# Turning the Xx blocks of a triangular inverse on VectorE instead of by TensorE products

## The chip, the cores and the metric

The kernel runs on one core of one Trainium2 chip. Times are device microseconds of that core. The engines are called as in the profile: PE is TensorE's matmul unit, PEld its weight load, DVE is VectorE, ACT is ScalarE, POOL is GpSimd, SP is SyncE.

## What is computed

Two model blocks run one after the other on 512 tokens of width 1024, everything in fp32. The first block (modulated norm, gated spatial unit, state space scan, feed forward) isn't touched by the change. The second block is:

```python
h = rmsnorm(x, norm_gain[l])
z = h @ w_in[l]
...
y_a = multi_scale_pool(u_a, pool_w[l], pool_scale[l])
y_b = rwkv7_time_mix(sh, w0[l], w_up[l], a0[l], a_up[l], k_k[l], k_a[l],
                     r_k[l], gn_gain[l], gn_bias[l]).astype(x.dtype)
y = jnp.concatenate([y_a * jax.nn.silu(g_a), y_b * jax.nn.silu(g_b)], axis=-1)
x = x + y @ w_out[l]
```

rwkv7_time_mix is a recurrence over the tokens for 8 heads of width 64:

```python
sa = jnp.einsum('bhvk,bhk->bhv', state, -kk_t)
state = (state * w_t[:, :, None, :]
         + sa[..., None] * (kk_t * a_t)[:, :, None, :]
         + v_t[..., None] * k_t[:, :, None, :])
y_t = jnp.einsum('bhvk,bhk->bhv', state, r_t)
```

The kernel computes it in chunks of 64 tokens. Within a chunk the recurrence needs the inverse of a unit triangular 64x64 matrix for each head and chunk, and the change is in how that inverse is built.

## The kernel before

**Big products.** Weights come in 128x1024 tiles through three buffers. ACT rounds a tile to whi (L1334), DVE takes the rest into wlo (L1881), and PE makes three products of 128x128 by 128x512 for each of eight k: L662, L663 and L664, below "the big products" (in the output projection they stand on L1225 to L1227). The weights are prepared two tiles ahead of their use.

**Side work.** Every engine's program is written out by hand in a fixed order and synchronised by semaphores. Each has two generators, side and main, and step() takes one step of side and then one of main. On PE a step comes after each k, so after three big products. On DVE and ACT the same number of steps is taken, with the tile's weight rounding (ACT) and split (DVE) put in after one of the first six steps. Because each queue is in order, an instruction that waits holds up all that stands behind it.

**The second block's stages.** There are four feature tiles f of 128 features (two heads of 64). While the big products of the six weight tiles of a window run, main prepares the keys of tile f (prep(f)) and side runs the recurrence of the tile before (rwkv). The last tile's recurrence runs beside the output projection. So rwkv comes four times, and the part with the inverse makes four stretches in the trace, called first to fourth here. In the second and third, DVE's side generator also finishes the norm of the tile before (norm_end: four reciprocals L2567, then L2570, L2575, L2580). In the second, DVE's main generator also scales XT eight times (x_scaled, L2341). Other DVE main work in the stretches is shift (L2357, L2359), L2398, L2401 and the reciprocals L2406.

**The inverse.** Xx holds the inverse so far: 16 matrices of 64x64 (two halves par of a pair of chunks, two heads h, four j), as a tile of 128x512. Row half par and column half h belong to (par, h). It starts as the identity with the first level merged in, so its diagonal blocks are 2x2. Five doublings q = 1 to 5 take the blocks to 64x64. Ln is the lower triangle of the matrix. In each doubling:

1. PE waits for the last merge (s_xx) and forms the 16 products of Ln and Xx in banks 3 and 4 (L1125).
2. PE turns Xx over by 16 products with the 64x64 identity I64, into banks 5 and 6 (L1133). In doubling 1 it first waits until the KA copies have been made (s_avc, s_avd), since KA's values lie in the same banks.
3. ACT copies the first result to Ww (L1760) and the second to Tt (L1763); each raises s_ww.
4. Two steps later PE waits for both copies and forms the 16 products of Tt and Ww in banks 3 and 4 (L1141). In doublings 1 and 2 four transposes (L1081) stand behind it.
5. DVE waits for that (s_lx) and merges the off-diagonal blocks of this level into Xx by a masked copy (L2481, called the merge here); it raises s_xx.
6. One step after L1141, PE's next doubling begins, or after the fifth the products of Xx and KA (L1152).

L2481 is the line of a helper: it also serves the masks of RB, Ln, AU and RK ahead of the doublings. L2511 is DVE's copy of half of KA, just ahead of the first doubling. L1028 (head sums for the keys) and L1034 (the pool's linear map) are products of PE's main generator that fall into the stretches.

Where an instruction reads what the one before wrote on the same engine, DVE waits on its own counter (own() raises s_dve).

Of the kernel before, what the change touches and what calls it, by code (L numbers as in the profile page):

```python
# [10 lines left out]
ACTF = mybir.ActivationFunctionType  # L11
# [23 lines left out]
def build_program(nc, A, out, blocks):  # L35
# [5 lines left out]
    def sem(name):  # L41
        return ctx.enter_context(nc.semaphore(name))
# [83 lines left out]
    Z = {n[0]: t for n, t in zip(names2, region(0, *names2))}  # L126
# [7 lines left out]
    PS = ctx.enter_context(nc.psum_tensor("PS", [P, 8, T], F32))  # L134
    BK = [PS[:, i, :] for i in range(8)]
# [99 lines left out]
    s_dve, s_act, s_pool = sem("s_dve_own"), sem("s_act_own"), sem("s_pool_own")  # L235
# [30 lines left out]
    s_rec, s_bo = sem("s_rec"), sem("s_bonus")  # L266
    s_nt, s_nat = sem("s_nt"), sem("s_nat")
    s_id, s_gr, s_gc, s_avc, s_avd = (sem(n) for n in ("s_id", "s_gram", "s_gcopy", "s_av_act", "s_av_dve"))
    s_lw, s_ww, s_lx, s_xx = (sem(n) for n in ("s_lw", "s_ww", "s_lx", "s_xx"))
    s_q, s_qa, s_qd, s_p, s_pv, s_pe = (sem(n) for n in ("s_q", "s_q_act", "s_q_dve", "s_p", "s_p_act", "s_p_dve"))  # L270
    s_s, s_sc, s_sb, s_y, s_yc = (sem(n) for n in ("s_s", "s_sc", "s_sb", "s_y", "s_yc"))
    s_gm, s_gmd, s_gs, s_gn = (sem(n) for n in ("s_gm", "s_gmd", "s_gs", "s_gn"))
# [16 lines left out]
    for q in range(32):  # L289
        g, j = divmod(q, 4)  # L290
# [345 lines left out]
    def pe_program(pe):  # L636
# [425 lines left out]
        def rwkv(f):  # L1062
# [55 lines left out]
            for q in range(1, 6):  # L1118
                n = 5 * f + q
                if q > 1:  # L1120
                    pe.wait_ge(s_xx, n - 1)
                    pe.wait_ge(s_ww, 2 * n - 2)
                for j in range(4):
                    for par, h in QUADS:
                        ms = pe.matmul(BK[3 + par][HALF[h], j * 64:(j + 1) * 64], mat(Ln, par, h, j), mat(Xx, par, h, j),  # L1125
                                       start=True, stop=True)
                ms.then_inc(s_lw, 1)
                if q == 1:
                    pe.wait_ge(s_avc, f + 1)
                    pe.wait_ge(s_avd, f + 1)  # L1130
                for j in range(4):
                    for par, h in QUADS:
                        ms = pe.matmul(BK[5 + par][HALF[h], j * 64:(j + 1) * 64], mat(Xx, par, h, j), I64[HALF[par], :],  # L1133
                                       start=True, stop=True)
                ms.then_inc(s_lw, 1)
                yield
                yield
                pe.wait_ge(s_ww, 2 * n)
                for j in range(4):
                    for par, h in QUADS:  # L1140
                        ms = pe.matmul(BK[3 + h][HALF[par], j * 64:(j + 1) * 64], matT(Tt, par, h, j), matT(Ww, par, h, j),  # L1141
                                       start=True, stop=True)
                ms.then_inc(s_lx, 1)
                if q <= 2:
                    pe.wait_ge(s_nat, 4 * f + 1 + q)
                    natural((lambda j: bt[:, j * 128:(j + 1) * 128], lambda j: kt[:, j * 128:(j + 1) * 128])[q - 1])
                yield

            pe.wait_ge(s_xx, 5 * f + 5)
            for j in range(4):  # L1150
                for par, h in QUADS:
# [162 lines left out]
    def act_program(act):  # L1314
# [423 lines left out]
        def rwkv(f):  # L1738
# [17 lines left out]
            yield  # L1756
            for q in range(1, 6):
                n = 5 * f + q
                act.wait_ge(s_lw, 2 * n - 1)
                act.activation(Z["Ww"][:, :].rearrange("p (a t) -> p a t", a=2), PS[:, 3:5, 0:256],  # L1760
                               ACTF.Copy).then_inc(s_ww, 1)
                act.wait_ge(s_lw, 2 * n)
                act.activation(Z["Tt"][:, :].rearrange("p (a t) -> p a t", a=2), PS[:, 5:7, 0:256],  # L1763
                               ACTF.Copy).then_inc(s_ww, 1)
                yield
                yield
                if q <= 2:
                    natural(f, 1 + q, Z[("Bn", "Kn")[q - 1]][:, :])
                yield
# [85 lines left out]
    def dve_program(v):  # L1855
# [3 lines left out]
        def own(ins):  # L1859
            nonlocal nown  # L1860
            ins.then_inc(s_dve, 1)
            nown += 1
# [617 lines left out]
        def masked(dst, mask, src):  # L2480
            return v.copy_predicated(two(dst[:, :]), mask[:, :].unsqueeze(1).unsqueeze(1).to_broadcast([P, 2, 4, 64]), src)  # L2481

        def rwkv(f):
            fx, KR, KA, QG, CS = Z[f"fx{f % 2}"], Z[f"KR{f % 2}"], Z["KA"], Z["QG"], Z["CS"]
            Xx, YT = Z["Xx"], Z["YT"]
# [3 lines left out]
            for i in range(REST if f == 0 else 0):  # L2489
# [3 lines left out]
            v.wait_ge(s_m2, N_MSK)  # L2493
            v.wait_ge(s_y, f)
            own(masked(Xx, MX[0], grams[:, :, :, 0, :]))
            masked(Z["RB"], M_U, grams[:, :, :, 1, :]).then_inc(s_gc, 1)
            v.wait_ge(s_gr, 4 * f + 2)
            masked(Z["Ln"], M_LO, pair(5)).then_inc(s_gc, 1)
# [11 lines left out]
            v.wait_ge(s_gr, 4 * f + 4)  # L2510
            v.tensor_copy(KA[64:128, :, :, 1, :], BK[6][64:128, :].rearrange("p (j h v) -> p j h v", j=4,  # L2511
                                                                             h=2)).then_inc(s_avd, 1)
            yield
            for q in range(1, 6):
                next(tail, DONE)
                yield
                next(tail, DONE)
                yield
                v.wait_ge(s_lx, 5 * f + q)
                masked(Xx, MX[q], pair(3)).then_inc(s_xx, 1)  # L2520
                yield
            v.wait_ge(s_q, f + 1)
            v.tensor_copy(QG[64:128, :, :, :, :].rearrange("p h j a t -> p h (j a t)"), PS[64:128, 5:7, :]).then_inc(s_qd, 1)
# [173 lines left out]
```

## Time and profile before

| what | value |
|---|---|
| median of 3 runs | 1439.01 us (1437.28 to 1439.88) |
| the profiled execution | 1438.04 us |
| its span | 1436.6 us |
| PE busy | 1419.0 us, 99% of the span |
| PEld busy | 1136.5 us, 79% |
| DVE busy | 886.0 us, 62% |
| ACT busy | 629.0 us, 44% |
| POOL busy | 213.8 us, 15% |

The span is the profiled execution on the core, from its first to its last instruction. The execution's own time is 1.4 us longer. Durations of matmuls overlap: from a group of matmuls to the next one counts the difference of their starts, not the busy time.

### The profile page before, as it was taken

The page shows a single profiled execution, that of the slowest core. Times are in us where ns is not written, and L with a number is a line of the kernel's source. Part 1 is how long each engine was busy: PE and PEld are TensorE (multiplying, and loading weights), DVE is VectorE, ACT ScalarE, POOL GpSimd, SP SyncE. Part 2 cuts the span into 40 slices and gives each one's busy share as a digit, 9 for nine tenths or more (in the row PEclk, how much of TensorE's full clock was granted, in tenths as well). Part 3 has the DMA queues.
Part 4 walks back from the last instruction along what each step waited for, and adds up shares of the span by engine and source line. Part 5 has one row for each costly group of instructions (what it writes and reads, how often), then busy time and mean ns, then how long its engine had stood idle before and what let it go on. Part 6 is the DMA issues. An engine that isn't in the chain of part 4 may idle for free.

```text
span 1436.6 us, 25193 instructions
## 1 busy us (share of the span) xinstructions
PE 1419.0 (99%) x9939; PEld 1136.5 (79%) x9939; DVE 886.0 (62%) x1248; ACT 629.0 (44%) x980; POOL 213.8 (15%) x238
## 2 busy tenths in 40 slices
PE   8999999999999999999999999999999999999998
PEld 4788888888788888888878888888888677777677
DVE  3777777778445677765556433344355865866736
ACT  4565655565554324322334322243334454444535
POOL 0000000000048898910006000000000000000200
PEclk9999999999999999999999999999999999999999
DMA  9454444443446675633323333333333221111111
GB/s 338 122 144 124 122 122 117 131 134 108 121 135 187 162 224 157 198 96 100 91 73 103 99 100 96 90 102 100 99 96 89 77 58 45 47 45 56 40 43 60
DMA packets 267356, 159.80 MB, mean 111 GB/s; under 512 B 5933, under 2 KB 255074, under 8 KB 267242
## 3 DMA queue, kind: packets, MB, share of 16 engines
q1 hardware_dynamic: 267242, 158.19, 37.8%
q8 instruction: 83, 1.36, 0.4%
q14 instruction: 31, 0.25, 0.1%
HBM read 155.92 MB, written 2.24 MB: 110 GB/s over the span
## 4 chain that ended last, share of the span: by engine, by line
PE 91%; DVE 5%; ACT 2%; issue 2%; POOL 0%; DVEq 0%; ACTq 0%; POOLq 0%
PE PS L662 24%; PE PS L664 23%; PE PS L663 23%; PE PS L841 1%; PE PS L911 1%; PE PS L867 1%; PE PS L912 1%; PE PS L913 1%; PE PS L1125 1%; DVE Hl L1893 1%; PE PS L1141 1%; PE PS L699 1%; PE PS L846 1%; PE PS L858 1%; PE PS L1133 1%
## 5 line engine op out<-in xcount | busy, mean ns | idle before, releaser
L662 PE MATMUL PS<-Hh,whi 128*128 128x512 f32 x1120 | 457.8, 409 | 0.6 <-ACT tmp L1383 0.3
L663 PE MATMUL PS<-Hl,whi 128*128 128x512 f32 x1120 | 436.8, 390 | 0.0
L664 PE MATMUL PS<-Hh,wlo 128*128 128x512 f32 x1120 | 436.7, 390 | 0.0
L1881 DVE TENSOR_TENSOR wlo<-raw,whi 128x1024 fp32r<-128x1024 f32 (+1 forms) x211 | 275.6, 1306 | 111.2 <-ACT whi L1334 110.7
L1334 ACT ACTIVATE whi<-raw 128x1024 fp32r<-128x1024 f32 (+1 forms) x211 | 221.2, 1049 | 166.9 <-PE PS L664 131.9
L662 PEld LDWEIGHTS PS<-Hh,whi 128*128 128x128 f32 x1120 | 210.4, 188 | 58.2 <-issue 14.6
L664 PEld LDWEIGHTS PS<-Hh,wlo 128*128 128x128 f32 x1120 | 210.3, 188 | 44.9
L663 PEld LDWEIGHTS PS<-Hl,whi 128*128 128x128 f32 x1120 | 210.6, 188 | 43.1 <-issue 4.1
L542 POOL TENSOR_TENSOR mbuf<-mbuf,cact 128x1024 f32<-128x1024 f32 x32 | 64.5, 2016 | 420.2 <-DMA mbuf<-in_w_mod_dram 416.5
L662 PE MATMUL PS<-YBh,whi 128*128 128x512 f32 x256 | 99.7, 389 | 0.0
L664 PE MATMUL PS<-YBh,wlo 128*128 128x512 f32 x256 | 99.6, 389 | 0.0
L663 PE MATMUL PS<-YBl,whi 128*128 128x512 f32 x256 | 99.6, 389 | 0.0
L547 POOL TENSOR_TENSOR mbuf<-mbuf 128x512 f32<-128x512 f32 x64 | 93.0, 1453 | 5.0
L629 POOL TENSOR_TENSOR pad<-pad 128x512 f32<-128x512 f32 x10 | 11.0, 1098 | 549.8 <-DVE VT L2359 543.8
L2022 DVE SCALAR_TENSOR_TENSOR tmp<-xr,pcA,tmp 128x512 f32<-128x512 f32 x96 | 71.8, 748 | 7.1 <-ACT tmp L1422 5.6
L2301 DVE TENSOR_TENSOR tmp<-tmp 128x512 f32<-128x512 f32 x32 | 22.2, 694 | 56.1 <-ACT tmp L1615 56.1
L664 PEld LDWEIGHTS PS<-YBh,wlo 128*128 128x128 f32 x256 | 48.1, 188 | 10.1
L662 PEld LDWEIGHTS PS<-YBh,whi 128*128 128x128 f32 x256 | 48.1, 188 | 9.9
L663 PEld LDWEIGHTS PS<-YBl,whi 128*128 128x128 f32 x256 | 48.1, 188 | 9.9
L1615 ACT ACTIVATE tmp<-PS 128x512 f32<-128x512 f32 x32 | 19.1, 597 | 74.9 <-PE PS L664 73.5
L662 PE MATMUL PS<-R2h,whi 128*128 128x512 f32 x128 | 50.2, 392 | 0.3 <-DVE modc L2047 0.3
L663 PE MATMUL PS<-R2l,whi 128*128 128x512 f32 x128 | 49.8, 389 | 0.0
(408 smaller groups left out, 2006.5 us busy)
## 6 DMA issues: line engine op xcount, KB each, us to landing
raw<-in_w_in_dram SPq DMA_DIRECT2D x106, 512.0 KB, 3.9
raw<-in_w_ff_dram SPq DMA_DIRECT2D x64, 512.0 KB, 3.8
mbuf<-in_w_mod_dram SPq DMA_DIRECT2D x32, 512.0 KB, 3.9
wm<-in_w_mod_dram SPq DMA_DIRECT2D x8, 1024.0 KB, 9.5
crow<-cum_rows SPq DMA_DIRECT2D x32, 256.0 KB, 4.6
raw<-in_w_branch_ssm_dram SPq DMA_DIRECT2D x16, 512.0 KB, 3.6
erow<-exp_rows SPq DMA_DIRECT2D x24, 256.0 KB, 5.1
raw<-in_w_out_dram SPq DMA_DIRECT2D x10, 512.0 KB, 3.5
```

What stands on the lines that cost most here:

```text
L542: pool.tensor_tensor(w[:, :, :], w[:, :, :], cact[:, :].unsqueeze(2).to_broadcast([P, KT, P]), ALU.mult).then_inc(s_pool, 1)
L547: pool.tensor_tensor(w[:, 0:n, :], w[:, 0:n, :], w[:, n:2 * n, :], ALU.add).then_inc(s_pool, 1)
L662: pe.matmul(bank[:, :], whi[s][:, k, :], xh[:, kk, :], start=kk == 0, stop=False)
L663: pe.matmul(bank[:, :], whi[s][:, k, :], xl[:, kk, :], start=False, stop=False)
L664: last = pe.matmul(bank[:, :], wlo[s][:, k, :], xh[:, kk, :], start=False, stop=t == end - 1 and k == (order or range(kt))[-1])
L699: pe.matmul(h4(BK[bank][:, :]), identb[:, :], identb[:, :].unsqueeze(1).to_broadcast([P, 4, P]), start=True, stop=True)
L841: ms = pe.matmul(to(a), xdt[n % 2][:, h * 64:(h + 1) * 64], dec[n % 2][:, h * 128:(h + 1) * 128], start=True, stop=c == 0)
L1334: act.activation(whi[s][:, 0:kt, :], raw[s][:, 0:kt, :], ACTF.Copy).then_inc(s_whi, 1)
L1615: act.activation(q[:, :], bank[:, :], ACTF.Relu).then_inc(s_relu, 1)
L1881: v.tensor_tensor(wlo[s][:, 0:kt, :], raw[s][:, 0:kt, :], whi[s][:, 0:kt, :].bitcast(F32), ALU.subtract).then_inc(s_wlo, 1)
L2022: e = v.scalar_tensor_tensor(out=a[:, :], in0=b[:, tap:tap + T], scalar=cw(tap, tile), in1=a[:, :], op0=ALU.mult, op1=ALU.add)
L2301: v.tensor_tensor(q[:, :], q[:, :], q[:, :], ALU.mult).then_inc(s_f2, 1)
```

## The change

DVE turns Xx over with its own transpose, which turns each 32x32 block in place. Ahead of doubling q the diagonal blocks of Xx have at most 32 rows, so turning 32x32 blocks turns the whole matrix over. Four instructions of 64 partitions by 256 columns write Tt from Xx directly, one for each (par, h), and move between partition halves on the way; they raise the new semaphore s_tt. The first set stands behind the KA copy (L2511), the others right behind the merges of doublings 1 to 4, on which they wait (s_xx). PE loses the 16 products L1133 of each doubling and waits for s_tt ahead of L1141. ACT loses the copy to Tt (L1763). PE's wait for the KA copies moves from doubling 1 to the products L1152.

```diff
--- before.py
+++ after.py
@@ -266,7 +266,7 @@
     s_rec, s_bo = sem("s_rec"), sem("s_bonus")
     s_nt, s_nat = sem("s_nt"), sem("s_nat")
     s_id, s_gr, s_gc, s_avc, s_avd = (sem(n) for n in ("s_id", "s_gram", "s_gcopy", "s_av_act", "s_av_dve"))
-    s_lw, s_ww, s_lx, s_xx = (sem(n) for n in ("s_lw", "s_ww", "s_lx", "s_xx"))
+    s_lw, s_ww, s_tt, s_lx, s_xx = (sem(n) for n in ("s_lw", "s_ww", "s_tt", "s_lx", "s_xx"))
     s_q, s_qa, s_qd, s_p, s_pv, s_pe = (sem(n) for n in ("s_q", "s_q_act", "s_q_dve", "s_p", "s_p_act", "s_p_dve"))
     s_s, s_sc, s_sb, s_y, s_yc = (sem(n) for n in ("s_s", "s_sc", "s_sb", "s_y", "s_yc"))
     s_gm, s_gmd, s_gs, s_gn = (sem(n) for n in ("s_gm", "s_gmd", "s_gs", "s_gn"))
@@ -1119,23 +1119,16 @@
                 n = 5 * f + q
                 if q > 1:
                     pe.wait_ge(s_xx, n - 1)
-                    pe.wait_ge(s_ww, 2 * n - 2)
+                    pe.wait_ge(s_ww, n - 1)
                 for j in range(4):
                     for par, h in QUADS:
                         ms = pe.matmul(BK[3 + par][HALF[h], j * 64:(j + 1) * 64], mat(Ln, par, h, j), mat(Xx, par, h, j),
                                        start=True, stop=True)
                 ms.then_inc(s_lw, 1)
-                if q == 1:
-                    pe.wait_ge(s_avc, f + 1)
-                    pe.wait_ge(s_avd, f + 1)
-                for j in range(4):
-                    for par, h in QUADS:
-                        ms = pe.matmul(BK[5 + par][HALF[h], j * 64:(j + 1) * 64], mat(Xx, par, h, j), I64[HALF[par], :],
-                                       start=True, stop=True)
-                ms.then_inc(s_lw, 1)
-                yield
-                yield
-                pe.wait_ge(s_ww, 2 * n)
+                yield
+                yield
+                pe.wait_ge(s_ww, n)
+                pe.wait_ge(s_tt, n)
                 for j in range(4):
                     for par, h in QUADS:
                         ms = pe.matmul(BK[3 + h][HALF[par], j * 64:(j + 1) * 64], matT(Tt, par, h, j), matT(Ww, par, h, j),
@@ -1146,6 +1139,8 @@
                     natural((lambda j: bt[:, j * 128:(j + 1) * 128], lambda j: kt[:, j * 128:(j + 1) * 128])[q - 1])
                 yield
 
+            pe.wait_ge(s_avc, f + 1)
+            pe.wait_ge(s_avd, f + 1)
             pe.wait_ge(s_xx, 5 * f + 5)
             for j in range(4):
                 for par, h in QUADS:
@@ -1756,11 +1751,8 @@
             yield
             for q in range(1, 6):
                 n = 5 * f + q
-                act.wait_ge(s_lw, 2 * n - 1)
+                act.wait_ge(s_lw, n)
                 act.activation(Z["Ww"][:, :].rearrange("p (a t) -> p a t", a=2), PS[:, 3:5, 0:256],
-                               ACTF.Copy).then_inc(s_ww, 1)
-                act.wait_ge(s_lw, 2 * n)
-                act.activation(Z["Tt"][:, :].rearrange("p (a t) -> p a t", a=2), PS[:, 5:7, 0:256],
                                ACTF.Copy).then_inc(s_ww, 1)
                 yield
                 yield
@@ -2480,6 +2472,16 @@
         def masked(dst, mask, src):
             return v.copy_predicated(two(dst[:, :]), mask[:, :].unsqueeze(1).unsqueeze(1).to_broadcast([P, 2, 4, 64]), src)
 
+        def turned(n):
+            Xx, Tt = Z["Xx"], Z["Tt"]
+            if n > 1:
+                v.wait_ge(s_lx, n - 1)
+            for par in range(2):
+                for h in range(2):
+                    e = v.transpose(Tt[64 * h:64 * h + 64, par * 256:par * 256 + 256],
+                                    Xx[64 * par:64 * par + 64, h * 256:h * 256 + 256])
+            e.then_inc(s_tt, 1)
+
         def rwkv(f):
             fx, KR, KA, QG, CS = Z[f"fx{f % 2}"], Z[f"KR{f % 2}"], Z["KA"], Z["QG"], Z["CS"]
             Xx, YT = Z["Xx"], Z["YT"]
@@ -2493,6 +2495,7 @@
             v.wait_ge(s_m2, N_MSK)
             v.wait_ge(s_y, f)
             own(masked(Xx, MX[0], grams[:, :, :, 0, :]))
+            inverse = nown
             masked(Z["RB"], M_U, grams[:, :, :, 1, :]).then_inc(s_gc, 1)
             v.wait_ge(s_gr, 4 * f + 2)
             masked(Z["Ln"], M_LO, pair(5)).then_inc(s_gc, 1)
@@ -2510,6 +2513,8 @@
             v.wait_ge(s_gr, 4 * f + 4)
             v.tensor_copy(KA[64:128, :, :, 1, :], BK[6][64:128, :].rearrange("p (j h v) -> p j h v", j=4,
                                                                              h=2)).then_inc(s_avd, 1)
+            v.wait_ge(s_dve, inverse)
+            turned(5 * f + 1)
             yield
             for q in range(1, 6):
                 next(tail, DONE)
@@ -2518,6 +2523,9 @@
                 yield
                 v.wait_ge(s_lx, 5 * f + q)
                 masked(Xx, MX[q], pair(3)).then_inc(s_xx, 1)
+                if q < 5:
+                    v.wait_ge(s_xx, 5 * f + q)
+                    turned(5 * f + q + 1)
                 yield
             v.wait_ge(s_q, f + 1)
             v.tensor_copy(QG[64:128, :, :, :, :].rearrange("p h j a t -> p h (j a t)"), PS[64:128, 5:7, :]).then_inc(s_qd, 1)
```

## Rows read from the trace of the kernel before

**Rows 1.** the page, part 1: busy us, share and instructions of each engine
```profile
PE 1419.0 (99%) x9939; PEld 1136.5 (79%) x9939; DVE 886.0 (62%) x1248; ACT 629.0 (44%) x980; POOL 213.8 (15%) x238
```

**Rows 2.** windows, the four stretches of doublings: length; busy PE, PEld, DVE, ACT, POOL; PEclk
```profile
1162.36:1185.09 22.73, 22.73 (x537) 16.74 (x536) 13.40 (x19) 10.13 (x18) 0.00 (x0) 1.00 0.17 49
1225.53:1249.44 23.91, 23.86 (x538) 17.25 (x537) 19.07 (x29) 12.06 (x22) 0.00 (x0) 1.00 0.17 47
1292.58:1316.49 23.91, 23.85 (x539) 17.24 (x538) 14.08 (x21) 12.05 (x22) 0.00 (x0) 1.00 0.16 44
1361.93:1383.79 21.86, 21.86 (x534) 16.36 (x533) 8.16 (x11) 8.83 (x15) 0.00 (x0) 1.00 0.23 65
```

**Rows 3.** timeline of PE, third doubling of the second stretch: start us, us, what
```profile
1235.82 0.69 PE L1125 MATMUL PS<-Xx,Ln 64*64 64x64 f32 x32
1236.34 0.65 PE L1133 MATMUL PS<-id,Xx 64*64 64x64 f32 x32
1236.91 0.50 PE L662 MATMUL PS<-Hh,whi 128*128 128x512 f32 x1
...
1238.50 0.69 PE L1141 MATMUL PS<-Ww,Tt 64*64 64x64 f32 x32
1239.12 0.50 PE L662 MATMUL PS<-Hh,whi 128*128 128x512 f32 x1
...
1240.05 0.69 PE L1125 MATMUL PS<-Xx,Ln 64*64 64x64 f32 x32
```

**Rows 4.** timeline of DVE, second stretch; in brackets the idle time before, its releaser
```profile
1225.41 0.69 DVE L2511 COPY KA<-PS 64x512 f32<-64x512 f32 x1
1226.13 0.75 DVE L2341 SCALAR_TENSOR_TENSOR XT<-XT,pcB,tmp 128x512 f32<-128x512 f32 x1
...
1229.67 0.73 DVE L2481 COPY_PREDICATED Xx<-msk,PS 128x512 f32<-128x512 uint8 x1
...
1234.67 0.74 DVE L2481 COPY_PREDICATED Xx<-msk,PS 128x512 f32<-128x512 uint8 x1 [0.24 <-PE PS L1141]
1235.30 0.47 DVE L2398 TENSOR_SCALAR acc<-wk,pcC 128x512 f32<-128x512 f32 x1
...
1239.26 0.73 DVE L2481 COPY_PREDICATED Xx<-msk,PS 128x512 f32<-128x512 uint8 x1 [0.37 <-PE PS L1141]
...
1248.65 0.74 DVE L2481 COPY_PREDICATED Xx<-msk,PS 128x512 f32<-128x512 uint8 x1 [1.04 <-PE PS L1141]
```

**Rows 5.** a group of DVE, whole span: busy us, mean ns | idle before, releaser
```profile
L2072 DVE TENSOR_TENSOR xdt<-xn,dts 128x256 f32<-128x256 f32 x32 | 13.5, 420 | 17.5 <-ACT xn L1463 17.5
```

**Rows 6.** timeline of DVE, first stretch, doublings one, four and five
```profile
1165.81 0.74 DVE L2481 COPY_PREDICATED Xx<-msk,PS 128x512 f32<-128x512 uint8 x1 [1.90 <-PE PS L1141]
...
1180.06 0.73 DVE L2481 COPY_PREDICATED Xx<-msk,PS 128x512 f32<-128x512 uint8 x1
...
1184.30 0.74 DVE L2481 COPY_PREDICATED Xx<-msk,PS 128x512 f32<-128x512 uint8 x1 [1.40 <-PE PS L1141]
```

**Rows 7.** timeline of DVE, third stretch, doublings one, two, three and five
```profile
1296.27 0.74 DVE L2481 COPY_PREDICATED Xx<-msk,PS 128x512 f32<-128x512 uint8 x1 [1.35 <-PE PS L1141]
...
1301.72 0.74 DVE L2481 COPY_PREDICATED Xx<-msk,PS 128x512 f32<-128x512 uint8 x1 [1.89 <-PE PS L1141]
...
1306.31 0.73 DVE L2481 COPY_PREDICATED Xx<-msk,PS 128x512 f32<-128x512 uint8 x1 [1.69 <-PE PS L1141]
...
1315.69 0.74 DVE L2481 COPY_PREDICATED Xx<-msk,PS 128x512 f32<-128x512 uint8 x1 [1.04 <-PE PS L1141]
```

**Rows 8.** timeline of DVE, fourth stretch, fourth and fifth doubling
```profile
1378.78 0.73 DVE L2481 COPY_PREDICATED Xx<-msk,PS 128x512 f32<-128x512 uint8 x1 [1.93 <-PE PS L1141]
...
1383.00 0.73 DVE L2481 COPY_PREDICATED Xx<-msk,PS 128x512 f32<-128x512 uint8 x1 [2.52 <-PE PS L1141]
```

**Rows 9.** windows at both ends of the span, columns as in Rows 2
```profile
0.00:20.00 20.00, 15.68 (x107) 9.09 (x108) 5.51 (x14) 10.65 (x17) 1.88 (x12) 1.00 0.95 321
1429.00:1431.00 2.00, 2.00 (x13) 2.00 (x11) 1.09 (x2) 2.00 (x4) 0.00 (x0) 0.55 0.33 130
```

## Prediction

> **What bounds the kernel now.** First the page's busy times: PE works in 1419.0 of a span of 1436.6 us, 99%, and DVE in 886.0, 62% [rows 1]. So whatever leaves PE's queue is worth its full time as long as nothing makes PE wait instead, and every wait that is new on PE is lost. The averages say nothing of the place of the change, so next come the windows cut to it: the four stretches from the first L1125 to L1152, one for each feature tile [rows 2]. PE is full in all four (22.73 of 22.73, 23.86 of 23.91, 23.85 of 23.91, 21.86 of 21.86 us). DVE differs: 13.40, 19.07, 14.08 and 8.16 us. The second stretch, in which DVE also runs the eight scalings of XT and the end of the first norm, has under 5 us to spare, the fourth over 13.
>
> Third, PE's timeline of one doubling [rows 3]. L1125 starts at 1235.82, the turning products L1133 at 1236.34, the first big product at 1236.91, L1141 at 1238.50, the next doubling's L1125 at 1240.05. Between L1141 and that L1125 stand only three big products, 1.55 us, and in this time DVE must have merged the result: its L2481 starts at 1239.26, 0.76 after L1141, takes 0.73 and ends at 1239.99 [rows 4], 0.06 before L1125. So **the merge (L2481 on Xx) has no slack**: a merge that starts late by x makes L1125, and the whole of PE, late by x. The idle time in brackets before each merge is what DVE can take on per doubling before that happens.
>
> **What goes.** Per doubling the 16 products of L1133. L1125 to L1133 is 0.52 us and L1133 to the big product 0.57, 1.09 together; straight from a 64x64 group to a big product takes 0.62 (L1141 at 1238.50, L662 at 1239.12) [rows 3]. The gain is 0.47 us a doubling, 20 times: 9.4 us if nothing waits. ACT loses 20 copies (L1763); its busy share is 44% [rows 1] and nothing on PE waited for them last, since they stood two big steps ahead of L1141. I count that at nothing, gain or loss. The first doubling's wait for KA's copies moves to L1152, some 20 us later, and is free. No DMA and nothing of SP or POOL moves.
>
> **What comes.** Per doubling four turns of 64x256 on DVE, 80 in all. The trace has no turn. The nearest row is a 128x256 operation, SBUF to SBUF, 420 ns [rows 5]. How they follow on each other counts as much. Ordinary neighbours overlap: the merge at 1234.67 takes 0.74, and the next starts after 0.63. But L2511, which works in partitions 64 to 127, started at 1225.41, took 0.69, and its successor on all 128 started at 1226.13, 0.03 after its end [rows 4]. The turns go (by output) to partitions 0, 64, 0, 64, so none overlaps: 0.45 each, **1.80 us for four**. The Trainium skill (VectorE: DVE Perf Modes, section Two Vector instructions with no wait between them) says the same of any instruction whose output starts in another quadrant than the last one's, and those rows agree; by no such rule the sum would be that of the first rival below. The same page's section The three transpose paths gives 311 ns for 128x128 in bf16; with 128 more columns at the row's rate that would be an estimate of 0.44 to 0.45 a turn, 0.02 to 0.03 more than I take.
>
> The first turn stands behind L2511 and adds 1.80. The others wait for the merge's own end (0.74+0.03 in place of 0.63, so 0.14 more) and add **1.94** each. All that stands behind them in DVE's queue is late by it, the next merge included.
>
> **Does L1141 wait for the turn itself?** The turn ends 0.77+1.80 = 2.57 after the merge starts, 2.67 with 0.1 for the signal. L1125 starts 0.79 after the merge (1239.26 to 1240.05), and L1141 follows after 2.68-0.47 = 2.21, so at 3.00. It does not, with 0.33 spare. In the first doubling of stretches two and three it may, by 0.3, which the late merge covers.
>
> **The sum.** Lateness of merge q against before is the larger of two: on PE's path the previous one less 0.47; on DVE's the previous one plus 1.94 (first: 1.80) less the idle time before that merge.
>
> Second stretch [rows 4]. Merge 1 has no idle before it: +1.80. Merge 2, 0.24 idle: +3.50. Merge 3, 0.37: +5.07. Before merge 4 DVE waits twice for PE, for L1028 and for L1141, and has more room than it needs, so PE's path decides: +4.60. Merge 5, 1.04: **+5.50**.
>
> First stretch [rows 6]. Merge 1, 1.90: -0.10. Two and three stand behind more idle time than 1.94+0.47 and go by PE: -1.04. Merge 4 had none, with reciprocals and a weight split before it: +0.90. Merge 5, 1.40: **+1.44**.
>
> Third stretch [rows 7]. 1.35: +0.45. 1.89: +0.50. 1.69: +0.75. Merge 4 by PE: +0.28. Merge 5, 1.04: **+1.18**.
>
> Fourth stretch. Three by PE, -1.41. Merge 4, 1.93 [rows 8]: -1.40. Merge 5, 2.52: -1.98 by DVE, -1.87 by PE: **-1.87**.
>
> Together +6.25 us. The lateness stays, since PE has nothing to catch up with, and DVE is no later against PE at each stretch's end than before. The profiled execution took 1438.04 us (span 1436.6 and 1.4 around it), the median of the three runs is 1439.01, so it stands 0.97 under it: 1444.3 against its own time, **1445.3 against the median**, 0.4% slower. A measurement of this kernel tells 0.2%, 2.9 us, from no change.
>
> **The rivals.**
> *The turns overlap.* If separate output halves do not hold them, each starts 0.36 after the last, 1.44 for four. The same recursion gives +0.36, +4.06, -0.26 and -2.23: +1.9 us, 1440.9, within 0.2%. Against it stands the 0.03 behind L2511; for it, that L2511 is one case. Chance 0.12.
>
> *The turns take two elements a cycle; faster.* L2398, from SBUF to SBUF with one source like a turn, takes 0.47 for 512 columns, where two sources take about 0.7 [rows 4]. Half of that saving for 256 columns, some 0.13, makes a turn 0.29, and with the overlap of 0.1 four take 0.76. DVE's queue then holds PE up only in the second stretch: -0.98, +1.34, -2.02, -2.35, in all -4.0 us, 1435.0. Four turns must take under 0.95 us for a gain over 0.2%; held but at this rate (1.28) the sum is +0.2. The Trainium skill's table of perf modes (same page) gives the double rate to copy and tensor_scalar and not to a shuffle, and does not list the turn. No run here shows it. Chance of a gain 0.10.
>
> *The turns are slow; much slower.* At half the rate in fp32 a turn takes 0.27 more, four 2.88. Then L1141 too waits for the turn, and a doubling costs at least 0.77+2.88+0.10+0.76 = 4.5 us against PE's 3.8. The recursion with this floor gives +5.9, +10.2, +5.5, +1.3: +23 us, 1462. Values between are likelier: at 2.40 for four it is +14, 1453. Chance 0.15, half of it below 1454.
>
> *PE's clock falls in the new gaps.* In the second stretch PE would stand for nearly 8 us of 30 (5.5 lost and 2.35 gained). In the first 20 us PE is busy 78% with a granted clock of 1.00; near the end it fell to 0.55 over two busy microseconds, after gaps [rows 9]. At 1.2 for 2.4 GHz each doubling in that state costs up to 3.8 us more: +4 to +10. Chance 0.03.
>
> **How the numbers follow.** The forecast, held turns of 0.42 to 0.50 us, keeps 0.60, and 1.80 to 2.04 for four gives +6.3 to +9.3. Slower by over 0.2%: 0.60+0.15+0.03 = 0.78. Within: 0.12. Faster: 0.10. The range runs from 1438.5 (held at the double rate, or overlapping turns a little shorter than 1.44) to 1454 (2.40 for four); it leaves out the faster rival and the slowest turns.
>
> **What would show it.** In the profile after: 80 turns of about 0.42 us on DVE, 0.45 apart; PE's busy time down by 9 us and its idle time up by 15, as L1125 and L1152 wait for L2481 (the lateness at a stretch's end plus the 2.35 us of products gone from it): nearly 8 us in the second stretch, 3 to 4 in the first and third, 0.5 in the fourth, which alone is shorter (by 1.9 us); no wait of L1141 for Tt beyond 0.3. It is wrong if the turns' spacing is under 0.3 or over 0.6 us, if L1141 waits for Tt in every doubling, or if the second stretch is no longer than before.

## The result, and the profile after

The changed kernel takes 1444.84 us (median of 6 runs, 1443.03 to 1446.87) against 1438.14 (median of 6, 1436.95 to 1440.01) before: a ratio of 1.0039, 95% interval 1.0029 to 1.0049, so +5.6 us with 4.2 to 7.0. The forecast was slower by 6.3 us, with 1438.5 to 1454. The profiled execution of the changed kernel took 1443.10 us, at the low end of its own runs, with a span of 1441.6, 5.0 over the span of before.

First the page's line of busy times, the answer to [rows 1]:

```profile
PE 1407.1 (98%) x9299; PEld 1124.5 (78%) x9299; DVE 920.8 (64%) x1328; ACT 619.6 (43%) x960; POOL 213.6 (15%) x238
```

PE has 640 records fewer and 11.9 us less busy time, DVE 80 instructions more and 34.8 us more, and the span is longer. Of the 11.9 us, 9.0 lie in the four stretches below, where PE's idle time grew from 0.1 to 15.0 us: the prediction had 9 and 15. The averages hardly moved (99 to 98%, 62 to 64%), which says again that they don't show the place.

The windows of the four stretches, from the first L1125 to the products with KA (now L1147), with the columns of [rows 2]:

```profile
1161.88:1185.78 23.90, 20.53 (x376) 14.43 (x376) 22.43 (x38) 7.70 (x13) 0.00 (x0) 1.00 0.16 46
1226.21:1255.51 29.30, 21.60 (x379) 14.86 (x378) 27.97 (x49) 9.72 (x17) 0.00 (x0) 1.00 0.13 37
1298.62:1323.63 25.01, 21.51 (x379) 14.84 (x378) 22.96 (x41) 9.72 (x17) 0.00 (x0) 1.00 0.15 42
1369.02:1389.08 20.06, 19.62 (x375) 14.05 (x374) 17.10 (x30) 6.39 (x10) 0.00 (x0) 1.00 0.18 51
```

In the first three DVE is now the full engine (22.43 of 23.90, 27.97 of 29.30, 22.96 of 25.01 us) and PE the one with gaps. In the fourth PE is still full, and this one alone became shorter. Against [rows 2] the stretches changed by:

| stretch | forecast, us | measured, us |
|---|---|---|
| first | +1.44 | +1.17 |
| second | +5.50 | +5.39 |
| third | +1.18 | +1.10 |
| fourth | -1.87 | -1.80 |
| sum | +6.25 | +5.86 |

The span grew by 0.9 less than this sum: the first L1125 came 0.48 us earlier (1161.88, was 1162.36), and the rest lies mostly after the fourth stretch. The two profiles differ there in PE's granted clock. In the one of before it is down at 743 us, in the one of the changed kernel nowhere ahead of 1439 us:

```profile
743.00:746.50 3.50, 3.50 (x15) 2.47 (x15) 0.54 (x2) 0.26 (x1) 0.00 (x0) 0.52 0.00 0
```

So the spans do not compare the change alone. The stretches do: the clock is 1.00 in all eight.

The group of the turns, and the waits of PE from 1160 us on (us in total, times, the longest):

```profile
L2481 DVE STREAM_TRANSPOSE Tt<-Xx 64x256 f32<-64x256 f32 x80 | 35.2, 440 | 1.5
```

```profile
PEld PS L1125 <- DVE Xx L2473: 17.1, 15, 2.9
PE PS L1125 <- DVE Xx L2473: 10.7, 7, 2.4
...
PE PS L1147 <- DVE Xx L2473: 3.6, 3, 1.3
```

A turn takes 440 ns. The new wait is where it was expected: the first products of a doubling, and those with KA, wait for the merge (the helper's line is now L2473), on the matmul's own side 10.7 and 3.6 us. L1134 (L1141 before) waited 0.5 us in all for Tt, in the first doublings of the second and third stretches:

```profile
1228.76 0.69 PE L1134 MATMUL PS<-Ww,Tt 64*64 64x64 f32 x32 [0.26 <-DVE Tt L2481]
```

How the lateness comes about is seen in DVE's timeline of the second stretch, beside [rows 4]:

```profile
1232.19 0.72 DVE L2473 COPY_PREDICATED Xx<-msk,PS 128x512 f32<-128x512 uint8 x1
1232.94 1.80 DVE L2481 STREAM_TRANSPOSE Tt<-Xx 64x256 f32<-64x256 f32 x4
1234.77 0.17 DVE L2382 TENSOR_TENSOR fx<-fx 128x7 f32<-128x7 f32 x1
...
1238.84 0.72 DVE L2473 COPY_PREDICATED Xx<-msk,PS 128x512 f32<-128x512 uint8 x1
...
1244.94 0.71 DVE L2473 COPY_PREDICATED Xx<-msk,PS 128x512 f32<-128x512 uint8 x1
...
1249.61 0.73 DVE L2473 COPY_PREDICATED Xx<-msk,PS 128x512 f32<-128x512 uint8 x1 [0.74 <-PE PS L1134]
...
1254.70 0.67 DVE L2473 COPY_PREDICATED Xx<-msk,PS 128x512 f32<-128x512 uint8 x1
```

The merge starts at 1232.19, four turns run from 1232.94 to 1234.74 with no overlap, and the next instruction starts at 1234.77: 2.58 us after the merge where it was 0.63 before. The next merge comes at 1238.84 with no idle time before it. What stood in front of it (scalings of XT, the norm, the shift) had filled DVE already. Counted from the stretch's first L1125, the five merges start 1.84, 3.49, 5.00, 4.51 and 5.37 us later than before (the fourth stood at 1244.42 there); the prediction had 1.80, 3.50, 5.07, 4.60 and 5.50. So not only the sum but each step of it came true here.

And PE's timeline of the third doubling, beside [rows 3]:

```profile
1239.61 0.69 PE L1125 MATMUL PS<-Xx,Ln 64*64 64x64 f32 x32 [2.44 <-DVE Xx L2473]
1240.23 0.50 PE L662 MATMUL PS<-Hh,whi 128*128 128x512 f32 x1
...
1241.82 0.69 PE L1134 MATMUL PS<-Ww,Tt 64*64 64x64 f32 x32
...
1245.71 0.69 PE L1125 MATMUL PS<-Xx,Ln 64*64 64x64 f32 x32 [2.30 <-DVE Xx L2473]
```

L1125 to L1134 is 2.21 us, 0.47 less than the 2.68 of before, as worked out, and then PE waits 2.30 us for the merge: 3.89 us from L1134 to the next L1125, where it was 1.55.

### The profile page after: what moved, and what is told of

Read it like the earlier page. It is cut to its first block, busy times and chain, and to the rows that moved or that the text cites. A ratio compares the mean times of both kernels' runs of the same rounds, so it can differ in the third digit from the quotient of the medians.

```text
span 1441.6 us, 24012 instructions
## 1 busy us (share of the span) xinstructions
PE 1407.1 (98%) x9299; PEld 1124.5 (78%) x9299; DVE 920.8 (64%) x1328; ACT 619.6 (43%) x960; POOL 213.6 (15%) x238
## 3 DMA queue, kind: packets, MB, share of 16 engines
HBM read 155.92 MB, written 2.24 MB: 110 GB/s over the span
## 4 chain that ended last, share of the span: by engine, by line
PE 85%; DVE 9%; issue 3%; ACT 3%; POOL 0%; DVEq 0%; ACTq 0%; POOLq 0%
PE PS L662 22%; PE PS L664 21%; PE PS L663 21%; PE PS L841 1%; PE PS L911 1%; PE PS L867 1%; DVE Tt L2481 1%; PE PS L912 1%; PE PS L913 1%; DVE Hl L1885 1%; DVE Xx L2473 1%; PE PS L846 1%; PE PS L858 1%; PE PS L699 1%; DVE wlo L1873 1%
## 5 line engine op out<-in xcount | busy, mean ns | idle before, releaser
L663 PE MATMUL PS<-Hl,whi 128*128 128x512 f32 x1120 | 436.8, 390 | 0.0
L663 PEld LDWEIGHTS PS<-Hl,whi 128*128 128x128 f32 x1120 | 210.6, 188 | 43.2 <-issue 4.1
L663 PE MATMUL PS<-YBl,whi 128*128 128x512 f32 x256 | 99.6, 389 | 0.0
L663 PEld LDWEIGHTS PS<-YBl,whi 128*128 128x128 f32 x256 | 48.1, 188 | 10.0
L663 PE MATMUL PS<-R2l,whi 128*128 128x512 f32 x128 | 49.8, 389 | 0.0
```

Of the source, the lines that this page charges most:

```text
L663: pe.matmul(bank[:, :], whi[s][:, k, :], xl[:, kk, :], start=False, stop=False)
```

## The experiments

Three theories. **Queue:** the loss is what the turns add in DVE's queue in front of the merges, and the recursion of the prediction gives its size. **Latency:** the loss is that PE waits for the turned Tt. **Small gain:** PE's products were worth less than 0.47 us each. All kernels were compared with the kernel before on the same chip (medians 1437.6 to 1438.4). "Stretches" are changes against [rows 2], from each kernel's profile.

### The turns left out

```diff
-            v.wait_ge(s_dve, inverse)
-            turned(5 * f + 1)
+            if f == 0:
+                v.wait_ge(s_dve, inverse)
+                turned(1)
...
-                if q < 5:
-                    v.wait_ge(s_xx, 5 * f + q)
-                    turned(5 * f + q + 1)
...
-                pe.wait_ge(s_tt, n)
+                pe.wait_ge(s_tt, 1)
```

> The change without DVE's turns, all but the first of the first tile: Tt keeps that first content, so what is left out is 19 of the 20 turns of Xx, while PE still loses L1133 and ACT its copy. Queue theory (PE's products were worth 0.47 us each, and all that the change gave back comes from the turns in DVE's queue): each of the four stretches is shorter than before by 2.35 us (first by up to that), in all 9.4 us, about 1429 against 1438. Rival, that the products were partly hidden and worth less: a gain of 5 us or less, and stretches shorter by 1 to 1.5.

Measured: ratio 0.9943 (0.9930 to 0.9955), -8.2 us. Windows of the four stretches:

```profile
1161.74:1182.73 20.99, 20.58 (x377) 14.44 (x376) 15.21 (x22) 7.69 (x13) 0.00 (x0) 1.00 0.19 52
1223.17:1245.45 22.28, 21.45 (x379) 14.82 (x378) 18.96 (x29) 9.61 (x17) 0.00 (x0) 1.00 0.18 49
1288.56:1309.97 21.41, 21.32 (x378) 14.81 (x378) 14.15 (x21) 9.60 (x17) 0.00 (x0) 1.00 0.17 49
1355.37:1375.01 19.64, 19.60 (x375) 14.05 (x374) 8.16 (x11) 6.38 (x10) 0.00 (x0) 1.00 0.26 73
```

The stretches changed by -1.74, -1.63, -2.50 and -2.22, in all -8.09. So the products were worth 0.47 us each where nothing else bound (4.72 us for the ten of the third and fourth), and "small gain" falls. But 9.4, the figure of my expectation and of the prediction's "if nothing waits", was not to be had in the first two: the recursion, which I had not applied to this case, gives -1.5 and -1.6 there. In the first stretch part of this is the one set of turns that this kernel still has: it holds the first merge. In the second stretch DVE had no idle time before the first merge and 0.24 and 0.37 before the next two, and PE can't come earlier than those merges. One more thing shows in the third stretch: its first doubling alone became 0.71 shorter. In the kernel before, L1133 starts 0.72 us after L1125 there (1292.58 and 1293.30) and not 0.52, since it waits for KA's copies. This wait went too; the prediction had called its move free and counted no gain.

### The turns beside the old products

The kernel before, with PE's products kept, and the 80 turns added into a tile that nobody reads. Each new wait is on DVE's own work; none is on PE.

```diff
+        def turned(n):
+            Xx, Tt = Z["Xx"], Z["T2"]
...
+                    v.transpose(Tt[64 * h:64 * h + 64, :],
+                                Xx[64 * par:64 * par + 64, h * 256:h * 256 + 256]).then_inc(s_tt, 1)
...
+                if q < 5:
+                    v.wait_ge(s_xx, 5 * f + q)
+                    turned(5 * f + q + 1)
```

> The kernel before, with its 16 products L1133 and ACT's copy kept, and the 80 turns added on DVE behind the same instructions as in the change, into a spare tile that PE never reads. So L1141 never waits for a turn. Queue theory: the merges are late by what stands in DVE's queue all the same. By the recursion without PE's 0.47 and with 1.83 us for four turns the stretches grow by 2.5, 6.1, 1.8 and 0.0 us, in all +10.4, about 1448. Rival, that the change loses through PE's wait for Tt (the turn's latency on the path): nothing waits for these turns, so about 0 to +2 us.

Measured: ratio 1.0087 (1.0073 to 1.0101), +12.5 us. **Latency falls**: nobody waits for these turns, and the loss is there all the same. The stretches grew by 3.49, 7.55, 1.70 and 0.03, against 2.5, 6.1, 1.8 and 0.0 forecast. The third and fourth fit to 0.1. The first two together are longer by 2.4 than the queue makes them, and the windows of the first three say why:

```profile
1163.93:1190.15 26.22, 24.28 (x537) 17.77 (x536) 22.52 (x38) 10.12 (x18) 0.00 (x0) 0.93 0.15 43
1230.63:1262.09 31.46, 25.65 (x539) 18.34 (x538) 27.96 (x49) 12.26 (x22) 0.00 (x0) 0.95 0.13 35
1305.21:1330.82 25.61, 24.00 (x539) 17.23 (x538) 22.87 (x41) 12.16 (x22) 0.00 (x0) 1.00 0.14 41
```

PE's granted clock, the third column from the end, is 0.93 and 0.95 there. In the timeline the fall comes right behind a wait for the merge:

```profile
1250.28 1.12 PE L1126 MATMUL PS<-Xx,Ln 64*64 64x64 f32 x32 [1.89 <-DVE Xx L2482]
1251.15 1.10 PE L1134 MATMUL PS<-id,Xx 64*64 64x64 f32 x32
1252.18 1.90 PE L1029 MATMUL PS<-tmp,bd 128*128 128x512 f32 x2
1253.27 1.04 PE L663 MATMUL PS<-Hh,whi 128*128 128x512 f32 x1
1254.14 0.40 PE L664 MATMUL PS<-Hl,whi 128*128 128x512 f32 x1
```

From L1126 to the second big product is 3.86 us where the same work took 2.29 before (L1125 at 1240.05 to L663 at 1242.34): 1.57 lost to the clock. Without it the second stretch is at +5.98, forecast +6.1. In the first stretch the fall comes in the fifth doubling, behind one wait of 1.94 us:

```profile
1184.39 0.69 PE L1126 MATMUL PS<-Xx,Ln 64*64 64x64 f32 x32 [1.94 <-DVE Xx L2482]
```

```profile
1185.50:1189.00 3.50, 3.50 (x36) 2.47 (x36) 2.77 (x5) 1.34 (x3) 0.00 (x0) 0.51 0.47 138
```

L1126 to L1142 took 3.95 us there in place of 2.68, and the last merge, which the queue alone would have held up, had 0.87 us of idle time in front of it: without the fall the stretch is at about +2.6, forecast +2.5.

### One wide turn

One turn of 128x512. It turns the same blocks without swapping the partition halves, so that part of the computation is changed.

```diff
-            for par in range(2):
-                for h in range(2):
-                    e = v.transpose(Tt[64 * h:64 * h + 64, par * 256:par * 256 + 256],
-                                    Xx[64 * par:64 * par + 64, h * 256:h * 256 + 256])
+            e = v.transpose(Tt[:, :], Xx[:, :])
```

> The change with one turn of 128x512 in place of four of 64x256: the same 32x32 blocks are turned, but the halves are not swapped between the partitions, so this part of the computation is changed. PE, ACT and all waits as in the change. Queue theory with one column a cycle: one turn takes about 0.71 us and adds 0.75 (0.89 behind a merge) in place of 1.83 (1.97); by the recursion the stretches change by -1.0, +1.3, -2.0 and -2.35 against before, in all -4.1, about 1434. Rival, that a turn costs by elements moved through the block and not by columns and instructions: it takes as long as the four together, 1.8 us, and the time stays at that of the change, 1444.

Measured: ratio 0.9962 (0.9949 to 0.9974), -5.5 us; stretches -1.09, +0.46, -2.46 and -2.23, in all -5.32. DVE's timeline in the second stretch:

```profile
1235.97 0.75 DVE L2351 SCALAR_TENSOR_TENSOR wk<-tmp,pcC,pad 128x512 f32<-128x512 f32 x1
1236.64 0.72 DVE L2473 COPY_PREDICATED Xx<-msk,PS 128x512 f32<-128x512 uint8 x1
1237.39 0.71 DVE L2479 STREAM_TRANSPOSE Tt<-Xx 128x512 f32<-128x512 f32 x1
1238.03 0.45 DVE L2390 TENSOR_SCALAR acc<-wk,pcC 128x512 f32<-128x512 f32 x1
```

The same blocks take 0.71 us in one instruction and 1.80 in four. The time goes by columns (712 ns for 512, 440 for 256) and instructions, and the wide turn also lets its successor start 0.64 us after it, 0.07 before its end, which the narrow ones, with outputs in alternating halves, do not. I had counted 0.75 for it. With 0.64 the recursion gives +0.9 for the second stretch in place of +1.3. Most of the other 0.4 lies in how idle time is counted: it runs from the end of the instruction before, but a merge that finds DVE busy starts 0.08 before that end (here 1236.64, where the one before ends at 1236.72). So DVE has 0.08 us more room than the bracket shows, at three merges of this stretch, some 0.25 in all. The third stretch gained 0.46 more than forecast: 0.2 of it is the wait for KA's copies, the rest these same two.

### Three turns by another layout

The column half of a matrix is h xor par instead of h in all tiles that take part, and the banks of the products that fill them likewise. The pieces that stay in their partition half then lie side by side.

```diff
-            mat = lambda t, par, h, j: t[HALF[par], h * 256 + j * 64:h * 256 + j * 64 + 64]
+            mat = lambda t, par, h, j: t[HALF[par], (h ^ par) * 256 + j * 64:(h ^ par) * 256 + j * 64 + 64]
...
+            v.transpose(Tt[:, 0:256], Xx[:, 0:256])
             for par in range(2):
-                for h in range(2):
-                    e = v.transpose(Tt[64 * h:64 * h + 64, par * 256:par * 256 + 256],
-                                    Xx[64 * par:64 * par + 64, h * 256:h * 256 + 256])
+                e = v.transpose(Tt[64 - 64 * par:128 - 64 * par, 256:512], Xx[64 * par:64 * par + 64, 256:512])
```

> The change with the matrices of Xx, Tt, Ww, Ln, AU, RB and RK stored in column half (h xor par) instead of h (the banks of the products that fill them likewise), so that the pieces which stay in their partition half lie side by side: one turn of 128x256 and two of 64x256 do what four did. The whole computation is kept. Queue theory: 0.44 + 2 x 0.45 and the gaps, 1.38 us a doubling in place of 1.83. By the recursion +0.2, +3.8, -0.5 and -2.3 against before, in all +1.3, about 1439.5. Rival, that the cost goes with what must be moved across the halves: no more than 1 us better than the change.

Measured: ratio 1.0021 (1.0012 to 1.0030), +3.0 us: better than the change by about 2.6, less than forecast by 1.7. The stretches changed by +0.20, +5.19, -0.69 and -2.22; all but the second are within 0.2 of the forecast. Its fourth doubling, in windows of the timeline (the wait, the slow part, what follows):

```profile
1243.00:1245.50 2.50, 0.71 (x3) 0.24 (x2) 2.50 (x4) 0.00 (x0) 0.00 (x0) 1.00 0.04 7
1245.50:1249.40 3.90, 3.83 (x38) 2.43 (x39) 2.78 (x6) 1.09 (x2) 0.00 (x0) 0.58 0.48 134
1249.40:1252.00 2.60, 2.57 (x47) 1.62 (x49) 0.91 (x2) 0.00 (x0) 0.00 (x0) 0.97 0.00 0
```

Again the granted clock, near its lower level of 1.2 GHz (0.58 with the edges), behind the waits of 2.01 and 1.85 us for the last two merges. L1125 to L1134 took 4.66 us there, 1.59 more than the 3.07 at full clock (3.54 before, less 0.47). Without that the second stretch is at +3.60, forecast +3.8. The rival (cost by what crosses the halves) falls: the first and third stretches gained as the recursion says.

### The XT scalings moved, in the change and alone

```diff
-                if f == 2 and s in (5, 6, 7, 8, 9, 12, 13, 14):
-                    x_scaled((5, 6, 7, 8, 9, 12, 13, 14).index(s))
+                if (f, s) in XT_AT:
+                    x_scaled(XT_AT.index((f, s)))
```

XT_AT is the list of (1, 42) to (1, 46) and (2, 43) to (2, 45).

> The change, with the eight scalings of XT on DVE moved out of the second stretch: five to the end of the window before (feature tile 1, steps 42 to 46) and three to the end of the window of tile 2 (steps 43 to 45), where DVE idles 5.6 and 4.4 us. The whole computation is kept. Queue theory: the second stretch then has the idle time of the third and grows by 1.3 us in place of 5.4; +2.3 us against before, about 1440. Rival, that the second stretch is long because of the waits of PE and the turns' latency there and not of what else stands in DVE's queue: it stays over 4 us longer than before.

> Control for the last one: the kernel before with the same move of the eight XT scalings and nothing else. Queue theory: the merges of before were in time with the scalings in the stretch, so nothing moves: within 0.5 us of before. Rival, that the scalings held something up in the kernel before too, so that the move is worth the same 4 us there.

Measured: with the change, ratio 1.0018 (1.0009 to 1.0027), +2.6 us; alone, 0.9998 (0.9989 to 1.0007). The second stretch with the change, and then the same stretch of the control:

```profile
1227.76:1252.77 25.01, 21.50 (x378) 14.84 (x378) 22.95 (x41) 9.72 (x17) 0.00 (x0) 1.00 0.15 43
```

```profile
1224.58:1248.50 23.92, 23.87 (x538) 17.24 (x538) 14.07 (x21) 12.05 (x22) 0.00 (x0) 1.00 0.17 47
```

Some 5 us of DVE work, worth nothing in the kernel before (+0.01 in this stretch), are worth 4.3 in the same stretch once the turns are there (+5.39 becomes +1.10, the third stretch's own +1.09). DVE's queue is the cause, and whatever else stands in it shares in it. The stretches of the change with the move sum to +1.57, 1.0 less than the ratio gives. Its profile has the first L1125 1.04 us later than before, behind a fall of the clock at 14 us, in a part that the move doesn't touch.

### Turns only where DVE had time

```diff
+DVE_TURNS = {(0, 1), (2, 4), (3, 4), (3, 1), (0, 3), (1, 4), (0, 2), (3, 3), (3, 2), (3, 5)}
...
+                if (f, q) not in DVE_TURNS:
...
+                            ms = pe.matmul(BK[5 + par][HALF[h], j * 64:(j + 1) * 64], mat(Xx, par, h, j), I64[HALF[par], :],
+                                           start=True, stop=True)
```

A pair is (feature tile, doubling), the tile counted from 0.

> Mixed: DVE turns Xx over (four turns as in the change) in doublings 1 to 3 of the first stretch, 4 of the second and third, and all five of the fourth, those in front of whose merge DVE had idle time enough; in the other ten the products L1133 and ACT's copy stay as before. The whole computation is kept. Queue theory, by the recursion: -1.0, -0.5, -0.5 and -1.8 us, in all -3.8, about 1434, faster than before. Rival, that the turns cost wherever they stand (by the wait of L1141, or by clock falls): no faster than before.

Measured: ratio 0.9987 (0.9978 to 0.9996), -1.9 us; the stretches -1.24, -0.37, -0.38 and -1.82, in all -3.81, as forecast. The other 1.9 us were lost outside them. In the profile the clock fell at 14 us, and the first L1125 came 1.56 later than before. It fell again ahead of the fourth stretch, behind PE's waits for Hl and for RB, and the way from the third stretch to the fourth took 1.62 longer:

```profile
1352.00:1355.00 3.00, 1.58 (x6) 0.67 (x4) 3.00 (x6) 2.99 (x6) 0.00 (x0) 1.00 0.35 104
1355.00:1359.00 4.00, 3.39 (x36) 2.77 (x37) 3.93 (x8) 0.67 (x1) 0.00 (x0) 0.57 0.12 37
```

Those waits are not the change's: the kernel before has the same wait of 1.44 us for RB, at a clock of 1.00 in its profile. In the profiles of the turns beside and of the three turns the clock fell at this place too, in the others not. Why is open. That these falls make up the 1.9 us of the median is likely and not shown, since one run of eleven was profiled.

### Everything together

Three turns a doubling, the scalings moved, and DVE turning in doublings 1 to 3, 2 to 4, 2 to 4 and 1 to 5 of the four stretches.

```diff
+DVE_TURNS = {(0, 1), (0, 2), (0, 3), (1, 2), (1, 3), (1, 4), (2, 2), (2, 3), (2, 4), (3, 1), (3, 2), (3, 3), (3, 4), (3, 5)}
...
+                if (f, s) in XT_AT:
...
+            v.transpose(Tt[:, 0:256], Xx[:, 0:256])
```

> All that should help together: three turns a doubling in the layout (h xor par), the XT scalings moved out of the second stretch, DVE turning in doublings 1 to 3 of the first, 2 to 4 of the second and third and all of the fourth stretch, PE's products in the other six. The whole computation is kept. Queue theory, by the recursion with 1.38 us: -1.4, -1.0, -1.0 and -2.3 us, in all -5.7, about 1432. With no wait of PE over a microsecond left, its granted clock should hold at 1.00 in the stretches. Rival, that part of the cost is fixed per turned doubling: no better than the mixed kernel with four turns.

Measured: 1433.07 us, ratio 0.9963 (0.9950 to 0.9975), -5.3 us, faster than both kernels.

```profile
1161.92:1183.34 21.42, 21.36 (x441) 15.37 (x440) 17.48 (x27) 8.67 (x15) 0.00 (x0) 1.00 0.19 52
1223.79:1246.62 22.83, 22.53 (x442) 15.86 (x442) 18.17 (x30) 10.70 (x19) 0.00 (x0) 1.00 0.17 48
1289.74:1312.57 22.83, 22.52 (x442) 15.86 (x442) 18.18 (x30) 10.69 (x19) 0.00 (x0) 1.00 0.16 46
1358.94:1378.56 19.62, 19.57 (x374) 14.05 (x374) 14.95 (x25) 6.39 (x10) 0.00 (x0) 1.00 0.20 55
```

PE is full again in all four, at a clock of 1.00, and DVE has 4 to 5 us to spare in each. The stretches changed by -1.31, -1.08, -1.08 and -2.24, in all -5.71, forecast -5.7.

## Why the prediction was right

**The gain.** 0.47 us a doubling off PE holds: L1125 to L1134 is 2.21 us, as worked out. The "9.4 us if nothing waits" overstates what was to be had, since in the first two stretches merges with little or no idle time before them hold PE to their own pace; without turns (but for one set) 8.1 came.

**The turn.** Taken at 0.45 us from start to start, four 1.80. Measured 0.440 each, 1.80 for four and 0.03 to the next, 1.83 in all. The Trainium skill's 311 ns for the 128x128 case (VectorE: DVE Perf Modes, section The three transpose paths) gave an estimate of 0.44 to 0.45 a turn's duration where the row gave 0.42, and it was the nearer one.

**No overlap.** That turns with outputs in alternating halves do not overlap came true, and the wide turn, whose successor starts 0.07 us before its end, shows the contrast. The rule of the Trainium skill on instructions whose output starts in another quadrant than the last one's (VectorE: DVE Perf Modes, section Two Vector instructions with no wait between them) agrees with both; turns that keep their quadrant and still are four were not tried.

**Where the loss arises.** L1134 was not to wait for Tt: 0.5 us in all. The merge was to be late by what stands before it in DVE's queue: each stretch came out within 0.3 us of its sum, the second as the worst and the fourth as the only gain. The turns beside the old products, the moved scalings with their control, and the mixed kernel each confirm the queue, and the turns beside exclude the latency: they are in nobody's way but DVE's own.

**The rivals.** The overlap and the double rate are excluded by the 440 ns and the 1.83. So is the half rate. The clock, to which I gave a chance of 0.03, did not fall in the stretches in the profile of the changed kernel, but the chance was too small: in two of the eight experiments it fell three times behind waits like the ones that the change makes, at up to 1.6 us a time. The prediction argued from 78% busy time at full clock in the first 20 us. In five of the experiments' profiles the clock fell in just that part, which no experiment touches, here with the three turns and then in the changed kernel:

```profile
14.00:18.00 4.00, 4.00 (x27) 2.07 (x26) 3.12 (x6) 0.00 (x0) 0.00 (x0) 0.58 1.11 371
```

```profile
14.00:18.00 4.00, 4.00 (x40) 1.71 (x41) 2.51 (x5) 0.38 (x1) 0.00 (x0) 1.00 1.11 371
```

So one profile at full clock was no proof. The changed kernel's runs spread over 3.8 us, with a mean granted clock of 0.999 at 1443.10 us and 0.994 at 1446.87. 0.994 is also the mean in the profile of the turns beside, which has four falls ahead of its end. Falls will take part in the slow end, but no profile of such a run says where.

**The sum.** 6.25 us forecast for the stretches, 5.86 measured, 5.6 by the ratio. The largest miss, 0.27 in the first stretch, is from merge 1: the recursion let it be as early as -0.10 only, and carried this on, though L1125 of doubling 2 had 0.35 us to spare behind that merge (it started at 1166.96 us, the merge had ended at 1166.55, and 0.06 is the usual distance). The merges of this stretch show it: the second and third came 0.85 and 1.32 us earlier than before, forecast 0.57 and 1.04.

## What to carry to other kernels

On an in-order engine, ask of moved work not what it lasts but what stands behind it in the queue, and take the idle time in front of each deadline, one deadline after the other: the larger of two lateness terms, carried on, gave the stretches of nine kernels to 0.3 us once the clock's falls were set apart, but for two of the wide turn's (0.8 and 0.5) and with the two of the turns left out that I worked out only afterwards. A move that loses as a whole may gain where that idle time is larger than the work: here ten or fourteen of the twenty doublings. And the control tells it best: work that costs nothing in one kernel (the XT scalings) may cost 4 us in the next.

## What the runs showed of the hardware that was not expected

PE's granted clock fell to half, its level of 1.2 GHz, in every one of the ten profiles, and not always in the same places. In the last 12 us of the span it fell in all. The falls ahead of them, each for 3 to 4 us:

| place | fell | stayed at 1.00 | PE's waits before |
|---|---|---|---|
| 14 us | one wide turn, three turns, turns beside, XT moved with the change, mixed | before, changed, turns left out, XT moved alone, everything together | 1.38 and 1.0 us where it fell, 1.38 and at most 0.4 in the other five |
| 743 us | before, everything together | the other eight | 0.27 us, the same in the changed kernel |
| a stretch, behind a late merge | turns beside (two stretches), three turns | changed, with waits up to 2.44 us | 1.94 us; 1.03, 2.04 and 1.89; 1.25, 2.01 and 1.85 |
| ahead of the fourth stretch | turns beside, three turns, mixed | the other seven | about 0.3, 0.6 and 1.4 us, the same in before and in the changed kernel |

The two falls worked out above cost 1.6 us each. A single wait of 1.94 us was enough in one place, and 2.44 and 2.30 us one after the other did nothing in another. What decides is open; to compare profiles, look at the clock of the whole span first and then compare stretches at equal clock. The Trainium skill (TensorE: Matmul & The Clock Gate, section Why this matters for your kernels) speaks of longer idle gaps than these as the ones to avoid; the traces here show falls behind shorter ones.
